# Seven of fifteen head units as plain fp32 products, the condition spread by TensorE, and a reordered tap chain

## What is computed

```python
cond = jax.nn.silu(c)                                  # c: (1, 2048)
mod = cond @ ada_w[i, s] + ada_b[i, s]                 # (2048) @ (2048, 6144)
shift, scale, gate = jnp.split(mod, 3, axis=-1)
h = rms_norm(x, norm_g[i, 0]) * (1.0 + scale) + shift
b_gate, c_gate, v = jnp.split(h @ w_in, 3, axis=-1)    # w_in: (2048, 6144)
u = dwconv_centred(c_gate * v, w_conv)                 # width 3 over the tokens
out = (b_gate * u) @ w_out
```

## Time and profile before

| | |
|---|---|
| median of 3 runs | 2604.27 us (2603.66 to 2606.34) |
| profiled execution | 2604.66 us |
| its span on the core | 2602.9 us, 1.76 us less than its time |
| TensorE busy | 2544.0 us, 98% of the span |
| VectorE, ScalarE, GpSimd busy | 2082.5, 1377.1, 623.4 us |
| granted TensorE clock, mean | 0.994 of full speed |
| DMA | 679.73 MB, 261 GB/s on average |

### The profile page before, as it was taken

How to read it: one execution, slowest core, us unless ns; L and a number is a source line. 1 busy time by engine, 2 the same in 40 slices (tenths; PEclk the granted TensorE clock), 3 DMA queues, 4 the chain that set the end, 5 groups by cost and what they waited for, 6 DMA issues and landing times.

```text
span 2602.9 us, 45356 instructions
## 1 busy us (share of the span) xinstructions
PE 2544.0 (98%) x15582; PEld 2255.9 (87%) x15582; DVE 2082.5 (80%) x2637; ACT 1377.1 (53%) x2149; POOL 623.4 (24%) x576
## 2 busy tenths in 40 slices
PE   7899999999999999999999999999999999999998
PEld 6789999888888888888788888888888888888887
DVE  7988998998989989758788898888899655555654
ACT  4544454544444444556677645776754454444454
POOL 0011132333343343320011042113323111121123
PEclk8999999999999999999999999999999999999999
DMA  9979997798988888746565598554589555555554
GB/s 396 416 290 368 369 378 291 280 352 310 335 331 334 330 328 327 256 167 199 186 195 194 195 346 292 192 194 159 169 286 336 191 189 187 190 187 186 192 183 141
DMA packets 163918, 679.73 MB, mean 261 GB/s; under 512 B 18720, under 2 KB 18976, under 8 KB 139072
## 3 DMA queue, kind: packets, MB, share of 16 engines
q1 hardware_dynamic: 163728, 677.75, 72.6%
q0 software_dynamic: 48, 0.13, 0.0%
HBM read 675.58 MB, written 2.23 MB: 260 GB/s over the span
## 4 chain that ended last, share of the span: by engine, by line
PE 88%; DVE 6%; DMA 2%; ACT 1%; issue 1%; DVEq 0%; POOL 0%; ACTq 0%; POOLq 0%
PE psm L1159 47%; PE psm L1162 23%; PE psm L1225 3%; PE psm L1227 3%; PE psm L1226 3%; DVE wl L1475 2%; DMA xs<-in_ada 1%; PE psm L1440 1%; PE psr L1199 1%; DVE adat L1488 1%; ACT wh L730 1%; DMA raw<-in_w 1%; DVE xs L1488 1%; PE psr L1393 1%; PE psr L1440 1%
## 5 line engine op out<-in xcount | busy, mean ns | idle before, releaser
L1475 DVE TENSOR_TENSOR wl<-raw,wh 128x1024 fp32r<-128x1024 f32 x854 | 1079.6, 1266 | 289.9 <-ACT wh L730 285.1
L730 ACT ACTIVATE wh<-raw 128x1024 fp32r<-128x1024 f32 x854 | 900.4, 1056 | 388.6 <-PE psm L1162 179.3
L1159 PE MATMUL psm<-hcat,wh 128*128 128x512 f32 x3120 | 986.4, 397 | 1.4 <-DVE pad L1790 1.4
L1162 PEld LDWEIGHTS psm<-hcat,wl 128*128 128x128 f32 x3120 | 586.1, 188 | 138.6
L1159 PE MATMUL psm<-hid,wh 128*128 128x512 f32 x2240 | 703.6, 395 | 0.2 <-DVE wl L1475 0.2
L1162 PE MATMUL psm<-hcat,wl 128*128 128x256 f32 x3120 | 613.3, 278 | 0.0
L1162 PEld LDWEIGHTS psm<-hid,wl 128*128 128x128 f32 x2240 | 420.8, 188 | 99.5
L1159 PEld LDWEIGHTS psm<-hcat,wh 128*128 128x128 f32 x3120 | 476.1, 189 | 7.4 <-issue 5.9
L1488 DVE CUSTOM_DVE_ANT_0 adat<-adat,cond 128x2048 f32<-128x2048 f32 x176 | 462.8, 2630 | 16.0 <-DMA adat<-in_ada 15.9
L1162 PE MATMUL psm<-hid,wl 128*128 128x256 f32 x2240 | 440.0, 278 | 0.0
L1159 PEld LDWEIGHTS psm<-hid,wh 128*128 128x128 f32 x2240 | 341.0, 189 | 0.4 <-DVE wl L1475 0.4
(11 more groups left out here) (257 smaller groups left out, 2579.2 us busy)
## 6 DMA issues: line engine op xcount, KB each, us to landing
raw<-in_w SPq DMA_DIRECT2D x866, 512.0 KB, 4.4
adat<-in_ada SPq DMA_DIRECT2D x176, 1024.0 KB, 6.5
dec<-running_sums SPq DMA_DIRECT2D x48, 256.0 KB, 5.9
xs<-in_ada SPq DMA_DIRECT2D x8, 1024.0 KB, 11.3
zs<-in_ada SPq DMA_DIRECT2D x8, 1024.0 KB, 11.5
normt<-running_sums SPq DMA_DIRECT2D x16, 256.0 KB, 4.8
x<-in_xT SPq DMA_DIRECT2D x4, 512.0 KB, 9.6
out<-x SPq DMA_DIRECT2D x4, 512.0 KB, 3.5
```

Source lines behind the costliest of these rows:

```text
L730: act.activation(wh[:, h % 4, :], raw[:, h % 4, :], ACT.Copy).then_inc(hi_done, 1)
L1159: pe.matmul(both, wh[:, h % 4, (k + i) * P:(k + i + 1) * P], src[:, kb + i, :, :], start=(kb + i == 0), stop=(kb + i == KB - 1), skip_grou ...
L1162: mm = pe.matmul(bank[:, T:2 * T], wl[:, h % 4, (k + i) * P:(k + i + 1) * P], src[:, kb + i, 0, :], start=False, stop=(kb + i == KB - 1), ...
L1475: dve.tensor_tensor(wl[:, h % 4, :], raw[:, h % 4, :], wh[:, h % 4, :].bitcast(F32), ALU.subtract).then_inc(lo_done, 1)
```

## The change

- **Whole slabs.** The units are kept in their order, but the blocks of the first seven (`WHOLE`) are packed into slabs of their own. In row kb they are made as one product each of `raw` (fp32, unsplit) and `hv` (fp32, unsplit). 14 of the 30 head slabs are such; `hi` and `lo` of these only count. Their `raw` buffer is free when `mm_done` counts them, no longer at `lo_done`. The other eight units of a row keep the three fp32r products; they fill 16 slabs.
- **The condition** comes as one row of 8 KB, and four fp32 matmuls with a row of ones copy it to all partitions in PSUM, from where ScalarE's Silu reads it. 6 warm-up matmuls stand where 24 stood.
- **Behind the head** ScalarE and VectorE start at `mm_done` 29 and no longer at 30; `hi(32)` stands behind the gate copies of j = 0 and 1; the split of slab 34 and the gate copy of unit 15 stand within the tap chain.

```diff
+WHOLE = 7
+WHOLE_BLOCKS = [(kb, n) for kb in range(KB) for n in range(WHOLE)]
+HEAD_STREAM, HEAD_WHOLE = [], set()
+for _kb in range(KB):
+    HEAD_STREAM.append([(_kb, n) for n in range(WHOLE, HEAD_UNITS)])
+    for _p in range(len(WHOLE_BLOCKS) // 8):
+        if WHOLE_BLOCKS[8 * _p][0] == _kb:
+            HEAD_WHOLE.add(len(HEAD_STREAM))
+            HEAD_STREAM.append(WHOLE_BLOCKS[8 * _p:8 * _p + 8])
+HEAD_PLACE = {b: (h, k) for h, slab in enumerate(HEAD_STREAM) for k, b in enumerate(slab)}
-WARM_HEAD = 24
+WARM_HEAD = 6
...
@@ SyncE: load_half, head
-                at_least(sp, mm_done if unsplit(h - 4) else lo_done, h - 3)
+                at_least(sp, mm_done if unsplit(h - 4) or whole(h - 4) else lo_done, h - 3)
-                sp.dma_start(cond[:, :], c.partition_broadcast(P)).then_inc(c_in, 16)
+                sp.dma_start(c_row, c).then_inc(c_in, 16)
...
@@ ScalarE: head (the chain behind it), conv
-                hi(At(HEAD_SLABS + 2))
-                act.wait_ge(mm_done, HEAD_SLABS)
+                act.wait_ge(mm_done, HEAD_SLABS - 1)
                 for j in range(HEAD):
+                    if j == HEAD - 2:
+                        act.wait_ge(mm_done, HEAD_SLABS)
                     act.activation(head_gate[j], head_sum("c", j), ACT.Copy).then_inc(head_c, 1)
                     if j == 1:
-                        hi(At(HEAD_SLABS + 3))
+                        hi(At(HEAD_SLABS + 2))
+                hi(At(HEAD_SLABS + 3))
                 act.sem_inc(copied, HEAD_UNITS)
                 for j in range(HEAD):
+                    if j == 3:
+                        hi(At(HEAD_SLABS + 4))
                     if j >= 2:
                         head_upper(j - 2)
                     act.wait_ge(sc_pad, j + 1)
                     middle(At(j))
+                    if j == 3:
+                        gate_copy(At(HEAD), At(HEAD_UNITS))
...
@@ TensorE: head
+                pe.wait_ge(c_in, 16)
+                for j in range(4):
+                    pe.matmul(spread_bank[j][:, :], ones[0:1, :], c_row[:, j * 2 * T:(j + 1) * 2 * T], start=True,
+                              stop=True, skip_group_check=True).then_inc(c_spread, 1)
...
+                for kb in range(KB):
+                    for n in range(HEAD_UNITS):
+                        h, k = HEAD_PLACE[kb, n]
...
+                        if n == 0:
+                            at_least(pe, h_full, kb + 1)
+                        if n == WHOLE:
+                            at_least(pe, h_lo, kb + 1)
+                            at_least(pe, lo_done, h + 1)
+                        if n < WHOLE:
+                            if k == 0:
+                                pe.wait_ge(raw_in[h % 4], h // 4 * 16 + 16)
+                            mm = pe.matmul(sums, raw[:, h % 4, k * P:(k + 1) * P], hv[:, kb % 4, :], start=first,
+                                           stop=after, skip_group_check=True)
+                        else:
+                            mm = block(sums, h, k, hcat[:, kb, 0, :], hcat[:, kb, 1, :], first, after)
+                        if k == 7:
+                            mm.then_inc(mm_done, 1)
...
@@ VectorE: head (the chain behind it), conv
-                dve.wait_ge(mm_done, HEAD_SLABS)
+                dve.wait_ge(mm_done, HEAD_SLABS - 1)
...
+                dve.wait_ge(mm_done, HEAD_SLABS)
                 for j in range(3):
                     head_gated(j)
+                    if j == 1:
+                        lo(At(HEAD_SLABS + 4))
+                    if j == 2:
+                        conv_summed(At(HEAD_UNITS))
                     head_pad(j + 2)
```

More of the change, by code:

```diff
@@ L102, in unsplit, with whole @@
     return not h.terms and h.c in UNSPLIT
+def whole(h):
+    return not h.terms and h.c in HEAD_WHOLE
 def behind(g):
@@ L281, in build @@
         raw_bank, pair_bank = psr[0:2], psy
+        spread_bank = psr
+        c_row = xd[0:1, :, :, :].rearrange("p a b c -> p (a b c)")
         head_gate = (ta[:, 0, :], ta[:, 1, :], th[:, 0, :], th[:, 1, :], tt[:, 0, :])
@@ L720, in hi @@
                     return
+                if whole(h):
+                    at_least(act, hi_done, h)
+                    act.sem_inc(hi_done, 1)
+                    return
                 if unsplit(h):
@@ L799, in first_norm @@
                     at_least(act, h_lo, k - 3)
+                    act.wait_ge(mm_done, HEAD_PLACE[k - 4, WHOLE][0] + 1)
                 at_least(act, mod0_done, 2 * k + 2)
@@ L843, in conv @@
                     peeled = not j.terms and jj.c == HEAD
-                    hi(v * 2 + 4)
+                    if not peeled:
+                        hi(v * 2 + 4)
+                        gate_copy(jj, v)
+                    hi(v * 2 + 5)
                     if peeled:
                         head_upper(HEAD - 2)
[L847 to L851, removed]
                         head_upper(HEAD - 1)
@@ L1236, in head @@
                 mm.then_inc(norm_sum, 1)
[L1237 to L1246, removed]
+                for kb in range(KB):
+                    for n in range(HEAD_UNITS):
+                        h, k = HEAD_PLACE[kb, n]
+                        sums = head_bank[n // 2][:, (n % 2) * T:(n % 2) * T + T]
+                        first, after = kb == 0 and n % 2 == 0, kb == KB - 1
+                        if n == 0:
[12 more added lines that the diff above has]
+                            mm.then_inc(mm_done, 1)
             def single(u, src, lag=1):
@@ L1466, in lo @@
                     return
+                if whole(h):
+                    at_least(dve, lo_done, h)
+                    dve.sem_inc(lo_done, 1)
+                    return
                 if unsplit(h):
@@ L1573, in head @@
                         dve.wait_ge(rinv, 1)
[L1574 to L1578, removed]
+                        for k in range(4):
+                            scaled(k)
                     if a >= 2 and a % 2 == 0:
@@ L1606, in conv @@
                     k = jj % 2
-                    lo(v * 2 + 4)
+                    if not peeled:
+                        lo(v * 2 + 4)
+                        conv_summed(v)
+                    lo(v * 2 + 5)
                     if peeled:
                         head_gated(HEAD - 2)
[L1610 to L1613, removed]
                         head_gated(HEAD - 1)
@@ L2035 @@
     head = np.asarray(sc_in_w[0]).reshape(KB, P, 3, KB, P)
-    head = np.stack([head[kb, :, "bcv".index(part), j] for kb in range(KB) for part, j in HEAD_ORDER])
+    head = np.stack([head[kb, :, "bcv".index(HEAD_ORDER[n][0]), HEAD_ORDER[n][1]]
+                     for slab in HEAD_STREAM for kb, n in slab])
     head = head.reshape(-1, 2, 8, P, P).transpose(0, 1, 3, 2, 4).reshape(-1, 2, P, HALF)
```

19 lines of the change are left out of this document (15 added, 4 removed).

## The result

The change makes the kernel slower: a median of 2612.34 us (2608.70 to 2616.81, 10 runs) beside 2604.50 (2603.38 to 2606.34, 10 runs). The ratio is 1.0028, with a 95% interval of 1.0020 to 1.0036. I had forecast 2603.2 and a range up to 2607. The profiled execution took 2616.81 us, 4.5 above the median, so its losses are a little larger than the usual ones; its span is 2615.1, where before's was 2602.9.

A forecast was written before the change was run, and what follows sets the result against it. TensorE is 98% busy, so only idle or slowed time up to unit 18, paced by head transfers, can be won: 2.6 us sooner, 1.5 lost to half clock, 1.1 gained; 2603.2 us, range 2599 to 2607.

The forecast's parts named there:

- The plain products: Head rows: records 0.216 us apart, a row 5.9 us instead of 5.4; 8 us more TensorE work, hidden below 7.52.
- The condition's row: Kernel start: 1 MB less queued, everything behind lands 2.3 us sooner; spreading is hidden, fewer warm-up matmuls cost nothing.
- sums at half clock: Kernel start: if the sums don't follow closely they add up to 3 us; late by 1.5 in the upper bound.
- Slots that TensorE frees: Late head: held slabs dry the queue, 0.6 us ahead of tile 31, 0.6 more ahead of slab 30; tile at 130.0.
- 2.0 must be in hand: Head's DMA queue: a lone slab takes 3.2 us, 1.25 for bytes, so 2.0 us of queued transfers avoid running dry.
- one dry spell relieves the next: Late head: shortfalls of 0.6 us (slab 28) and 1.0 (slab 30) don't add; 0.6 falls first, then 0.6 more.
- The last row: End of the head: starts at 134.2 us (before 136.37), not waiting for the lower part; unit 15 at 140.2, not 143.72.
- Behind the head: Slab 32 and tap chain: first head_gated 1.8 us sooner, unit 18 at 163.6, 2.6 sooner; the pause moves there, 4.2 us.
- The clock: Unit 18: the 4.2 us pause ahead brings 3 us at half clock, losing 1.5; bounds 0 and 1.7.
- the one called slower: Head rows 9 to 14: four half-clock spells each hold a slab 1.7 us longer, drying the queue; 2610 us, chance 0.10.
- The other rival: Tap chain: L1619 ready at 159.4 lets unit 18 go, all three pauses vanish; 7 to 8.5 us gained, 2596, chance 0.10.
- The bounds: Whole kernel: 2599.5 to 2606.5 us; never-dry queue and no throttling below, throttled last row and late sums above.

The follow-up runs named there:

- e5: The changed kernel with eight buffers of their own for the whole slabs, so their loads don't wait on shared buffers; 2603.41 us, ratio 0.9997.
- e10: The changed kernel with three buffers of their own for the whole slabs; 2603.49 us, ratio 0.9997.
- e8: The kernel before with the condition spread by matmuls over 128 rows, 127 of them zero, started later; 2608.47 us, ratio 1.0014.
- e3: The kernel before with only the seven plain units (14 whole slabs); condition, warm-up and tail as before; 2610.11 us, ratio 1.0022.
- e1: The kernel before with only the new order of ScalarE and VectorE behind the head; 2604.36 us, ratio 0.9999.
- e11: e6 with four junk matmuls of 512 columns behind unit 17 and 20 warm-up matmuls, for the same instruction count; 2602.38 us, ratio 0.9991.
- e6: The changed kernel with own buffers for whole slabs, and the old start (broadcast condition, 24 warm-up matmuls); 2603.08 us, ratio 0.9994.
- e7: The changed kernel with SyncE issuing each ada tile a+1 ahead of slab a-1; 2611.86 us, ratio 1.0030.
- e12: The changed kernel, buffers still shared, with the old start (broadcast condition, 24 warm-up matmuls); 2608.97 us, ratio 1.0019.
- e4: The kernel before, all slabs split, but loads four slabs behind the same 14 slabs wait for TensorE's count, not VectorE's; 2638.86 us, ratio 1.0133.
- e9: e6 with 14 junk matmuls of 128 columns behind unit 17, thus more instructions; 2607.16 us, ratio 1.0010.
- e2: The kernel before with only the condition's row, four spreading matmuls and 6 warm-up matmuls for 24; 2605.74 us, ratio 1.0006.

## Why the prediction was wrong

- **The plain products**: right. Their records stand 0.216 us apart at full clock, as counted, and with own buffers the 8 us more of TensorE's work are hidden (e5, e10).
- **The condition's row**: the mechanism of the transfer was right (tile 1 lands 2.2 us sooner), "cost nothing" was wrong. I took half clock into the bounds of the spread, but let the clock rise by it; the 12 warm-up records and the sums then ran partly at half clock (6.21 us for 24 records, 5.45 in e8), and VectorE starts on `rbc` 1.5 us later than before (21.02 for 19.48). I had named that case (sums at half clock), but kept it for the bounds (1.5 us) and out of the sum. By the medians this is 0.9 us alone and 3.6 in the changed kernel; the intervals don't set either clearly apart from noise.
- **Slots that TensorE frees**: this is the step that failed. I saw the mechanism, found the place, and sized it at 1.2 us, with nothing ahead of slab 26. Alone it measured 5.3 (e3), and between the changed kernel and e5, which keeps all but the hold, 8.9. By the traces it makes tile 31 9.8 us late (141.9, and 132.1 in e5): some 2 of these by 44 us and 8 from there on, most of it ahead of slab 26. Two terms were wrong. The first is "2.0 must be in hand", which came from a lone slab. In the changed kernel a slab issued with 2.5 us still to land ahead of it (112.12) lost 1.4, one with 2.0 (130.65) 1.4 over its first two transfers, one with 4.2 (81.78) 1.1, one with 3.0 (95.21) 0.9 with the tile behind it, one with 4.0 (120.38) nothing at first. So about 4 us are wanted in a loaded queue; that is an estimate from rows that scatter. The in-hand figures themselves came out near for the last two held slabs (2.0 and 0.9 where I had 1.4 and 1.0). The second is that one dry spell relieves the next. In e3 the slabs issued at 99.05, 115.41 and 124.15 had 2.6, 2.5 and 2.7 in hand, though the queue had lost 1.3 us between the first and the second and 1.4 between the second and the third: nothing was given back. My reading is that a row that starts late ends late and frees its slab late by as much. Tile 31 came at 141.9 in place of 130.0.
- **The Trainium skill**, page "DMA: Bandwidth & Descriptors", section "Anatomy of one DMA", puts the fixed part of a transfer at about 2.0 us for DMAs of GpSimd's path, most of it completion. The lone slab of SyncE agrees with that (3.2 us less 1.25 for its bytes), and I took it for what a full queue wants. The rows above ask for more there, and they decide.
- **The last row**: 146.58 and not 134.2; it follows tile 31. That it starts without waiting for the lower part was right. It fell into a spell at half clock (granted clock 0.53 from 147.5 to 151), which I had as a bound (1.7).
- **Behind the head**: right in the terms that the traces give. Unit 15 starts without a pause, unit 17 waits 1.27 us for `lo` (I had 1.5), unit 18 3.90 (4.2). From the first `head_gated` (158.76) to the product that lets unit 18 go (176.99) are 18.2 us, where I had 18.4. From the last row's start to unit 18 are 30.9, where I had 29.4, the row's half clock being the difference.
- **The clock**: the mechanism was right, and is shown by taking the cause away: with the pause filled unit 18 starts at the same time (163.22 and 163.28) and runs at full clock. So the pause costs nothing itself. The half clock behind it takes 1.7 by the granted clock (e1). Downstream less of that is left: at 523.47 e11 starts the product that e6 starts at 524.97, and 0.3 of these 1.5 us are another, shorter pause.
- **The rivals**: the one called slower, at 2610 and 0.10, was the nearest in time and in its chain (slabs held longer by slow rows), but with the wrong start: it wanted four throttled spells first. The queue needed none. In the changed kernel the clock is full from 31.4 to 137.1 us, and the queue runs dry there all the same, as it does in e7 (the stretches are shown there) and in e12 (share 0.91 from 120 to 140 at full clock); throttling came on top at the end. The other rival, a chain that lets unit 18 go early, stays refuted by the 3.90 us.
- **The bounds**: the lower end of the forecast, 2599.5, doesn't follow from its terms; 1.2 and 1.5 below 2603.2 is 2600.5. Nothing hangs on it here.

## What to carry to other kernels

When an edit hands the release of a buffer from an engine that runs ahead to the one that runs last, count the in-order queue behind that one wait, not the one transfer: everything behind it comes late, and what must be in hand is read from a loaded queue, not from a lone transfer. The test is cheap: move only the wait (e4) or give these loads buffers of their own (e10; three were enough). And price a pause on TensorE by the clock behind it. Junk matmuls in the pause take the half clock away, but measure the whole kernel: four of them were worth 0.7 us, which is within the noise (e11), and 14 shorter ones made it 4.1 us slower (e9).

## What the runs showed of the hardware

- Matmuls that contract one partition did not raise TensorE's clock: 7.16 us of them back to back stayed at 1.2 GHz, where the same eight records with 128 rows were at 2.4 GHz before their end (5.07 us). After one-row spreading the clock rose at 12.9 us (e2), 14.3 (the changed kernel) and 16.1 (e5), after warm-up matmuls alone at 7.8 (before). The Trainium skill, page "TensorE: Matmul & The Clock Gate", part 1, says that activity releases the throttle. Here TensorE was busy by the trace, and the clock stayed low; the measurement decides. The stretches' granted clock reads 1.00 in these first microseconds; the records' durations are what tells it.
- The scatter is larger where slabs are held: the changed kernel's ten runs spread over 8.1 us, those of e3 over 7.4, those of before over 3.0, those of e10, without the hold, over 4.5. That fits a feedback; the seven runs of e7, also held, spread over 3.6 only.
- 14 more instructions on TensorE brought a pause of 4.10 us some 630 us further on (e9), which the same fill in four instructions didn't (e11). The instruction queue moved nine packets more in e9, four of them around the pause. What TensorE waits for there isn't shown.
